# The first tile's sum of expert outputs: gates as diagonal matrices on TensorE, and tile 0 scaled before tile 1 is added

## The reference, cut to what matters

```python
# end of the first block
x = x + g2 * moe(h)                    # moe: sum over 4 experts of gate * (expert(h) @ w2 + b2)
x = rms_norm(x, final_g)
# start of the second block
h = rms_norm(x, g_norm) * (1 + scale) + shift
proj = h @ w_in                        # x_rnn, z_rnn, q, k, v, z_attn, g_r, g_a
```

## Time and profile before

| | us |
|---|---|
| median of 3 runs | 1996.19 |
| lowest and highest | 1994.83, 1996.49 |
| profiled execution | 1998.96 |
| its span | 1997.7 |
| TensorE busy | 1937.8 (97% of the span) |
| VectorE busy | 836.2 (42%) |
| ScalarE busy | 424.7 (21%) |
| GpSimd busy | 240.0 (12%) |

### The profile page before, as it was taken

One profiled execution on the slowest core, in us unless ns is written; L12 is line 12 of the kernel. 1 busy time (PEld: TensorE's weight loads), 2 busy tenths in 40 slices (PEclk: granted clock), 3 DMA queues, 4 the chain that ended last, 5 costly groups with the idle time before them and its releaser, 6 DMA issues.

```text
span 1997.7 us, 38345 instructions
## 1 busy us (share of the span) xinstructions
PE 1937.8 (97%) x16481; PEld 1079.1 (54%) x16481; DVE 836.2 (42%) x1530; ACT 424.7 (21%) x914; POOL 240.0 (12%) x173
## 2 busy tenths in 40 slices
PE   8999998999999999999999999989999999999998
PEld 4455544433434434343443433345588888888887
DVE  5989875211121211121120211105458678654465
ACT  3223512210111110011010111102233443431102
POOL 0000000000000000000000000002244334360011
PEclk8999998999999999999999999998999999999999
DMA  8475796999799999999999999975112112122221
GB/s 339 139 282 195 286 335 268 420 419 366 319 421 419 420 420 419 421 419 420 419 419 420 418 420 416 419 295 225 63 68 89 67 67 89 66 85 85 85 85 64
DMA packets 103419, 553.94 MB, mean 277 GB/s; under 512 B 14224, under 2 KB 25488, under 8 KB 48336
## 3 DMA queue, kind: packets, MB, share of 16 engines
q1 hardware_dynamic: 81344, 516.84, 64.1%
q10 hardware_dynamic: 14848, 17.82, 2.7%
q0 software_dynamic: 7056, 16.79, 2.3%
HBM read 532.91 MB, written 26.35 MB: 280 GB/s over the span
## 4 chain that ended last, share of the span: by engine, by line
PE 72%; DMA 13%; SPq 10%; DVE 3%; issue 2%; ACT 1%; another core or an unknown queue 0%; ACTq 0%; DVEq 0%
PE psum L1112 24%; PE psum L926 19%; DMA arena<-in_w 9%; SPq L467 9%; PE psum L934 9%; PE psum L597 7%; PE psum L1071 3%; DMA ring<-in_w 2%; DMA arena<-in_mod_slabs 1%; PE psum L919 1%; PE psum L1199 1%; PE psum L1218 1%; PE psum L942 1%; PE psum L906 1%; PE psum L781 1%
## 5 line engine op out<-in xcount | busy, mean ns | idle before, releaser
L926 PE MATMUL psum<-arena,ring 128*32 128x512 f32 x4096 | 452.7, 596 | 11.3 <-DMA arena<-in_w 10.8
L926 PEld LDWEIGHTS psum<-arena,ring 128*32 128x32 f32 x4096 | 134.3, 110 | 310.1 <-issue 307.1
L2114 DVE TENSOR_SCALAR h_t<-psum 128x512 f32<-128x512 f32 (+2 forms) x33 | 27.9, 845 | 572.5 <-PE psum L926 572.5
L934 PE MATMUL psum<-arena,h_t 128*32 128x256 f32 x3840 | 217.9, 380 | 4.2 <-DMA arena<-in_w 3.3
L1458 ACT ACTIVATE ring<-psum,mods,gain 128x64 f32<-128x64 f32 (+2 forms) x264 | 85.6, 429 | 607.5 <-PE psum L906 607.5
L934 PEld LDWEIGHTS psum<-arena,h_t 128*32 128x32 f32 x3840 | 120.7, 110 | 101.1 <-issue 18.7
L2435 POOL DMA_INDIRECT ring<-h_rows,row_i x33 | 35.5, 1075 | 1144.0 <-PE psum L906 834.9
L1112 PE MATMUL psum<-ring 128*128 128x256 f32 x768 | 171.1, 379 | 0.0
L1112 PEld LDWEIGHTS psum<-ring 128*128 128x128 f32 x768 | 145.9, 190 | 20.1 <-issue 0.3
L1112 PE MATMUL psum<-h_t,ring 128*128 128x256 f32 x672 | 154.3, 379 | 0.2 <-ACT arena L1532 0.2
L926 PE MATMUL psum<-ring 128*32 128x512 f32 x1344 | 148.8, 593 | 5.5 <-DMA ring<-in_w 5.4
(11 more groups left out here) (480 smaller groups left out, 2132.6 us busy)
## 6 DMA issues: line engine op xcount, KB each, us to landing
arena<-in_w SPq DMA_DIRECT2D x288, 1024.0 KB, 30.9
ring<-in_w SPq DMA_DIRECT2D x96, 1024.0 KB
ring<-in_pairs SPq DMA_DIRECT2D x40, 1024.0 KB, 4.8
ring<-in_dot_slabs SPq DMA_DIRECT2D x40, 512.0 KB, 5.9
ring<-in_mod_slabs SPq DMA_DIRECT2D x6, 2048.0 KB, 9.2
ring<-in_proj_slabs SPq DMA_DIRECT2D x24, 512.0 KB, 4.4
y_rows<-arena SPq DMA_DIRECT2D x3, 3584.0 KB, 25.0
y_rows<-work ACTq DMA_DIRECT2D x70, 64.0 KB, 7.7
```

What stands on the lines that cost most here:

```text
L926: mm = pe.matmul(psum[32 * j:32 * j + 32, g, :], x_e[:, c * tokens + g * TG:c * tokens + g * TG + TG], slot[s][:, j * S:(j + 1) * S], star ...
L934: mm = pe.matmul(psum[32 * j:32 * j + 32, 6 + g // 2, (g % 2) * 256:(g % 2) * 256 + 256], h_e[:, g * 256 + half * P + 32 * c:g * 256 + hal ...
L2114: dve.tensor_scalar(gate, psum[:, 0:groups, 0:256], LIMIT, None, ALU.min).then_inc(sem("gate clipped"), 1)
```

## The change

Tile 0's weighted sum is no longer made by VectorE. VectorE makes four diagonal matrices (the identity times the column of gates of part k) in `by_gate`, which lies in the buffer `x_g[1]` that the expert stage used for gathered tokens, and TensorE multiplies each part of tile 0 with its diagonal, all four adding up in the same PSUM banks (`turn_parts`, 32 products in place of 8). The three groups of idle products in this place are gone. On VectorE tile 0 is scaled before any addition of tile 1. On TensorE `v_rows(0, 0)` comes before `turn_sum(1)`, and `norm_sums(1)` stands between the fourth and the fifth product of `v_rows(0, 1)`. ScalarE keeps V's first rows of tile 0 before the squares of tile 1.

```diff
+        by_gate = x_g[1][:, 0:TOPK * P].rearrange("p (k n) -> p k n", k=TOPK)
...
+            def turn_parts():
+                a = SUM_AT[0]
+                pe.wait_ge(sem("gates laid out"), TOPK)
+                for part in range(TOPK):
+                    pe.wait_ge(sem(f"first parts {part} gathered"), 16)
+                    for k in range(KT):
+                        mm = pe.matmul(psum[:, a + k // 4, (k % 4) * P:(k % 4 + 1) * P], parts[:, part, k * P:(k + 1) * P], by_gate[:, part, :], start=False, stop=(part == TOPK - 1), skip_group_check=True)
+                        if part == TOPK - 1 and k % 4 == 3:
+                            mm.then_inc(sem("sum turned"), 1)
+
             def turn_sum(t):
                 a = SUM_AT[t]
-                pe.wait_ge(sem("parts summed"), t + 1)
+                pe.wait_ge(sem("parts summed"), t)
...
-            def v_rows(t, i):
+            def v_rows(t, i, between=None):
...
+                    if between and k == 3:
+                        between()
                 mm.then_inc(sem("v product"), 1)
...
             second_bias(2)
-            keep_on(6, 0)
-            turn_sum(0)
-            keep_on(2, 0)
+            turn_parts()
             norm_sums(0)
-            keep_on(2, 0)
             spread_scale(0)
+            v_rows(0, 0)
             turn_sum(1)
-            v_rows(0, 0)
-            norm_sums(1)
-            v_rows(0, 1)
+            v_rows(0, 1, lambda: norm_sums(1))
             spread_scale(1)
...
+            keep_v_rows(0, 0)
             tile_squares(1)
-            keep_v_rows(0, 0)
             tile_root(1)
...
             def add_part(t, k):
                 acc = parts[:, t * TOPK, :]
-                if t == 0:
-                    dve.wait_ge(sem(f"first parts {k} gathered"), 16)
-                elif k == 0:
+                if k == 0:
                     dve.wait_ge(sem(f"parts {t} gathered"), 16 * TOPK)
...
+            dve.wait_ge(sem("x turned"), NP)
             for k in range(TOPK):
-                add_part(0, k)
+                dve.tensor_scalar(by_gate[:, k, :], identity, gates[:, 0, k:k + 1], None, ALU.mult).then_inc(sem("gates laid out"), 1)
             residual(0)
-            for k in range(3):
+            tile_scale(0)
+            tile_scaled(0)
+            for k in range(TOPK):
                 add_part(1, k)
-            tile_scale(0)
-            add_part(1, 3)
-            tile_scaled(0)
             residual(1)
```

## The result

The changed kernel takes 2006.34 us (median of 7 runs, 2000.93 to 2008.82) against 1998.24 (median of 7) for the kernel before beside it: ratio 1.0038, 95% interval 1.0023 to 1.0053. It is slower by 0.4%, where 1990.5 us was forecast, and the end lies outside the range. The span of the profiled execution is 2006.4 us.

A forecast was written before the change was run, and what follows sets the result against it. TensorE's queue was taken to bound the kernel; the sum, prompt signals, new order and new wait brought the landmark 5.7 us earlier, 1998.96 to 1993.3 us, carried to the median as 1990.5; range 1988.0 to 1996.8.

The forecast's parts named there:

- The sum of tile 0: Moving tile 0's sum from VectorE to 32 TensorE products, ending at 1357.0 against 1357.93: worth only 0.9 us.
- The two late signals: TensorE's signals for tile 0's residual and root, late behind streaming idle products; removing these gains nearly all of 2.4 and 3.5 us.
- the first rival: Signals stay late, held up by the gathers' traffic, not by idle products: landmark 0.4 us later, 1996.6 us; chance 0.24.
- The row of tile 2: Tile 2's norm sums end at 1400.28, root starts at 1400.32; used as evidence that signals without idle products behind are prompt.
- the row of tile 1: Tile 1's turned sum ended at 1373.05, VectorE took it at 1373.09; cited as prompt in the same traffic.
- The second rival: The clock falls during tile 0's new sum and stays down: 5.3 us more, 2001.5 us; chance 0.06.
- landmark: Start of tile 2's turned sum on TensorE: 1389.79 before, forecast 1384.1, 5.7 us less.
- The order after it: Tile 0 scaled before tile 1's additions: V's first products start at 1362.5, V's first half ends at 1372.5.
- a new wait: At tile 1's spreading product TensorE waits 1.1 us for VectorE; landmark 11.6 us after V's first half ends.

The follow-up runs named there:

- e2: Kernel before without the two pairs of idle products around tile 0's norm sums: 1997.26 us, ratio 1.0000 to the kernel before.
- e1: Changed kernel with tile 0's sum made again by VectorE, new order kept, idle products still out: 1993.9 us, ratio 0.9984 to the kernel before.
- e13: Kernel before, unchanged, traced again on a chip that showed no hold-up: 1990.0 us, ratio 1.0000.
- e3: Changed kernel with the gathers of tiles 1 to 3 held until tile 0's sum is turned: 1996.01 us, ratio 1.0005 to the kernel before.
- e5: Changed kernel with tiles 1 to 3 loaded directly from ScalarE's queue instead of gathered: 1994.02 us, ratio 0.9986 to the kernel before.
- e16: Changed kernel with the 12 gathers of tiles 1 to 3 replaced by direct loads on GpSimd's queue: 1991.45 us, ratio 0.9970 to the kernel before.
- e18: Changed kernel with the 12 gathers of tiles 1 to 3 fetching 1 KB rows, not 4 KB: 2001.84 us, ratio 1.0030 to the kernel before.
- e14: Changed kernel, unchanged, traced again on the chip that showed no hold-up: 1992.14 us, ratio 1.0000 to the kernel before.
- e8: Changed kernel with 15 idle products added ahead of TensorE's register load: 2005.28 us, ratio 1.0040 to the kernel before.
- e10: Changed kernel with the 12 gathers replaced by direct loads on GpSimd's queue, on the chip without hold-up: 1989.78 us, ratio 0.9996 to the kernel before.
- e15: Kernel before with the 12 gathers replaced by direct loads on GpSimd's queue, on the chip without hold-up: 1987.85 us, ratio 0.9986.
- e17: Changed kernel with the 12 gathers of tiles 1 to 3 naming consecutive rows: 2004.31 us, ratio 1.0047 to the kernel before.
- e7: Changed kernel with the gathers of tiles 1 to 3 held until tile 0's part 3 has landed: 1996.92 us, ratio 1.0007 to the kernel before.
- e6: e1 with the gathers of tiles 1 to 3 held until tile 0's part 3 has landed: 1992.58 us, ratio 0.9986 to the kernel before.

## Why the prediction was wrong

Two steps failed: "The sum of tile 0" in its cost, which is what made the kernel slow, and "The two late signals" in its cause.

**"The two late signals"** are late because GpSimd's indirect gathers are being issued, on the chips that show it, and not because idle products stream behind: e2 and e1 have none there and are late by 4.8 and 1.8 us, e13 has them and is late by nothing, e3, e5 and e16 lose the lateness with the gathers. In the changed kernel both signals came on time, as forecast, but that was luck: the sum had outlasted the last issue by 8.5 us (1363.64 to 1372.15). I had the first rival's condition right (signals stay late because of the gathers), but its reason, their traffic, falls with e5 and e18, and its price with what follows. The row of tile 2, where nothing was late, was put down to the V products that follow there; it was a row from after the gathers. So was the row of tile 1 that I set against the rival: 1373.09, where the last issue of before ends at 1366.01 (1364.40 + 1.61).

**"The sum of tile 0"** was costed at the rate of a turned sum in quiet time, 1.78 us for eight products. That is the right size without gathers: e3 had 2.05 and 1.87 us for 16 records. But the window in which TensorE's signals are late by 2.4 and 3.5 us is also one in which products can be held up, and I moved 24 into it. The rows of before gave no price for that: short runs go through there unharmed (the turned sum's 16 records in 2.05 us; in e1, at a clock of 0.50, 3.78 and 3.57 us), and the run of 64 is held up only behind its first 21 to 40 records. It took 18.6 us and not 7.96. How the excess of 10.6 divides can't be told from one trace: the holes themselves are 4.5 us, while e14, without the hold-up and at a clock of 0.50 at the start of its sum and 1.00 at its end, took 10.05, 8.5 us less. By e8, which began at full clock and took 22.2, the hold-up is enough by itself. VectorE's four operations had gone through the same gathers unharmed: in e1 the last one ends at 1352.02 and the turned sum starts at 1352.08.

**The clock** fell ahead of the place where I looked. In the stretch before the bias TensorE idles at the register load in both kernels (3.01 us before, 3.10 in the changed one); with that idle the clock fell in the changed kernel's trace (0.50 in 1344 to 1348, the bias 7.17 us) and did not in the first one of before. Of the 4.5 us by which the sum began late, 3.25 are the bias at this clock and 1.3 a later start of it, because the two idle products ahead took 3.75 us for 2.00 at this clock. The second rival, "falls during the new sum and stays down", comes nearest in time with 2001.5 us. Its price for a sum at half clock, 14.2 us, was sound: the last 25 records, all at 0.50, took 5.68 us, which makes 14.5 for 64. What it lacked was the hold-up and the slower bias, and its clock did not stay down: it fell early, rose and fell again. By e8 this clock was not what made the kernel slow, since the gathers set the end anyway.

**The sum of it:** landmark 1398.46 against 1384.1, 14.4 us: 4.5 late start, 10.6 longer sum, and 0.8 us less than forecast behind it. **"The order after it"** and **"a new wait"** were right: 0.83 us for 1.1, 11.58 for 11.6, V's first half 9.63 us for 9.97. In e16 nearly the forecast path appears, 39.8 us for 39.5, in part by luck: V's products started 19.8 us after the first gather where 17.9 were forecast, and V's first half took 8.4 for 10.0. And where nothing is held up the change gains next to nothing: with direct loads 39.8 us (e16) and 43.7 (e10) against 40.3 (e15), with gathers 43.7 (e14) against 42.7 (e13).

Of the two pages of the Trainium skill that bear on this, "TensorE: Matmul & The Clock Gate", per-tile semaphore tail, has products complete in program order and a signal trail its product by some tens of nanoseconds, and names no delay from what is queued behind. That agrees with e13 (0.04 us, idle products behind), and there I had departed from it; with gathers under way the traces disagree with the size, by 1.6 to 4.8 us. "DMA: Bandwidth & Descriptors", section on SWDGE and HWDGE, describes one way for all DMAs issued from GpSimd, direct and indirect, and names interference with VectorE only. That one shows here too: beside VectorE's additions of 128x1024 two issues of before took 1.61 us in place of 0.94. But e16 and e17 differ by 11 us between the two kinds of DMA, and on TensorE.

**Open:** what in an indirect gather reaches TensorE, why VectorE and ScalarE show nothing of the kind, and why one chip is free of it. The first 8 to 16 us after the first gather have no holes (0.49 us in e17 between the products of part 0 and of part 1 may be the wait for part 1), and no run told what starts them. The profile models the ends of products, so a signal that comes late can't be told from a last product that ends late. The holes have a step of their own: in all five traces the pieces of the sum behind them start 0.7, 1.4, 2.1 or 2.8 us apart (1360.80, 1362.93, 1363.63, 1365.75, 1366.47 above), at either clock, while the gathers are issued every 1.25 us. V's products of 512 columns show no holes: in e7 they run from 1363.17 in one piece while gathers are still issued.

## What to carry to other kernels

A signal that comes late by microseconds with no releaser is a property of that engine in that window until an experiment says otherwise; work moved onto the engine there pays it once per wait and, as here, once per few instructions, so don't price it by a row from a quiet stretch. A short row from the same window isn't enough either: the turned sum stood there with 2.05 us and gave no warning; the late signals were the only one, and a trial run the only price. Keep TensorE work, above all long runs of short products, out of the time in which indirect gathers are issued, or load directly where the rows allow it. And where a few microseconds decide, look at a second trace of the kernel before, on another chip: the first one showed late signals that another chip does not have.

## What the runs showed of the hardware

- While GpSimd issues indirect gathers (0.94 us each, one every 1.25 us, up to 1.61 each beside VectorE's additions), a run of 32 products of 128x128 breaks up behind its first 21 to 40 records into pieces of one to four with holes of up to 1.73 us, at granted clocks of 1.00 and 0.50 alike, and some of TensorE's signals come up to 4.8 us late; runs of 16 records and V's products of 512 columns show no holes; in the five traces with the diagonal sum among unheld gathers the last hole ends 2.8 to 3.0 us after the last issue, while the late roots of e1, e6 and e7 came before it. Order and size of the rows hardly matter.
- Direct loads of 512 KB on the same queue are issued faster (12 in 6.36 us) and showed no hold-up in e10, e15 and e16, of which only e16 ran on a chip that may have it; from ScalarE's queue they showed none on a chip that has it (e5).
- One chip of those used showed none of it in any of its five traces with indirect gathers, and the unchanged kernel is 0.2 to 0.4% faster there; that the second comes from the first is not shown.
